# A decoder step on one Trainium2 core: the query tiles of the prompt attention in another order

## The chip, the core and the metric

The kernel runs on one core of one Trainium2 chip. The metric is the device time of one execution in microseconds (us); of several executions the median counts. The core has five engines with queues of their own: PE (TensorE, matrix products; PEld is its weight load), DVE (VectorE), ACT (ScalarE), POOL (GpSimd) and SP (SyncE, here only a queue of DMA transfers). They run side by side and wait for one another through semaphores.

## The reference

One step of a one-layer decoder on a prompt of 1024 tokens and on 8 sampled tokens with 4096 past positions each. The part that the change touches is the sparse attention of the prompt (8 query heads of 64 elements, 2 key-value heads), three branches over the same queries, mixed by gates. Since the prompt has 16 blocks of 64 and the 16 best are chosen, the selected branch is plain causal attention here.

```python
def masked_softmax(s, mask):
    s = jnp.where(mask, s.astype(jnp.float32), -1e30)
    m = jnp.max(s, axis=-1, keepdims=True)
    e = jnp.where(mask, jnp.exp(s - m), 0.0)
    return e / jnp.maximum(jnp.sum(e, axis=-1, keepdims=True), 1e-30)

def win_attend(qg, q_pos, k, v, k_pos, slopes):
    dist = (q_pos[:, None] - k_pos[None, :]).astype(jnp.float32)
    mask = (k_pos[None, :] >= 0) & (dist >= 0) & (dist <= WINDOW)
    s = jnp.einsum('bhgtd,bshd->bhgts', qg, k).astype(jnp.float32) * (NSA_HEAD_DIM ** -0.5) - slopes[None, :, :, None, None] * dist
    p = masked_softmax(s, mask)
    return jnp.einsum('bhgts,bshd->bhgtd', p.astype(v.dtype), v)

def nsa_merge(g, o_cmp, o_slc, o_win, dtype):
    o = g[0] * o_cmp + g[1] * o_slc + g[2] * o_win
```

`cmp_attend` (63 compressed rows) and `sel_attend` (all keys up to the query) have the same form. No query tile needs the result of another.

## The kernel before, in words

The program is a row of phases: load and norm, input projection, the gated linear attention, then `phase_attend` (the prompt's sparse attention, line 1594), `phase_sample` (the 8 sampled tokens, with the output projection in its last part) and the feed-forward phase. `phase_attend` and what follows it share one block, so each engine goes on to the sample phase as soon as its own queue of the attention is empty; between the phases before them all engines meet.

**Units.** The 1024 queries are 8 tiles of 128. A unit is one query tile `qt` with one pair of heads `gp`, twice, for both key-value heads; there are 16 units, two per query tile, in the order of the tuple `order_qt` (line 1610). `SU` lists them. Unit n has `ls = (qt + 1) * 128` selected keys, `lw` window keys (up to 640) and 63 compressed ones. That makes 319, 575, 831, 1087, 1343, 1471, 1599 and 1727 columns per head for `qt` 0 to 7, in (`tiles`, line 1638) 3, 5, 7, 9, 11, 12, 13 and 14 tiles of keys, and in (`chunks`, line 1619) 2, 2, 2, 3, 4, 4, 4 and 4 groups of score columns for each of the two g.

**What happens to a unit.** PE multiplies queries with keys (`score`, L1852). DVE adds the slope's distances, copies the scores from PSUM to SBUF and takes maxima (`reduce`, L1789 to L1800). ACT takes exponentials and sums (`exps`, L1726). DVE turns sums and gates into weights (`weigh`, L1809 to L1812). POOL multiplies the first key-value head's probabilities with them (L1707), ACT the second's (L1750). PE turns the probabilities tile by tile (`turn`, L1867), ACT and DVE move the turned tiles alternately out of PSUM (L1737, L1819), PE multiplies them with the values (`values`, L1880), ACT moves the result to `hT` (L1742), and SP stores it (L1697).

**Stages.** All engines walk the same loop `for n in range(-2, NSU)`. In stage n, PE turns and multiplies unit n while it scores unit n + 2; ACT meanwhile does the second half of the exponentials of unit n + 1 and the first half of unit n + 2. The work of the unit ahead is dealt out over the `J = stages(n)` steps of unit n by `share`. The turning of unit n + 1 waits for the last weighing of that unit on POOL (`normd`) and on ACT (`norma`), which is the last thing ACT does in stage n:

```python
            if j == 0:
                pe.wait_ge(normd, 2 * n + 2)
                pe.wait_ge(norma, 2 * n + 2)
```

Stages -2 and -1 have nothing to turn: they are the opening, with the scores of units 0 and 1 alone. Stages 14 and 15 have nothing to score: they are the close. In the close POOL also issues three gathers of cache rows for the sample phase (`gather_rows`, L1585), two of them behind a wait for the last turning of unit 13, and so ahead of the last two weighings. SP issues one twelfth of a copy of the cache (`pack_blocks`) ahead of each of its first 12 stores.

Of the kernel before, what the change touches and what calls it, by code (L numbers as in the profile page):

```python
# [1593 lines left out]
def phase_attend(nc, M, A, O, block):  # L1594
# [12 lines left out]
    sm = M.misc[:, 712:712 + 6 * NSLOT].rearrange("p (s b k) -> p s b k", s=NSLOT, b=3)  # L1607
    rc = M.misc[:, 736:736 + 6 * NSLOT].rearrange("p (s b k) -> p s b k", s=NSLOT, b=3)

    order_qt = (1, 3, 5, 7, 6, 4, 2, 0)  # L1610
    SU = [(qt, gp) for qt in order_qt for gp in range(2)]
    NSU = len(SU)

# [1879 lines left out]
def build(nc, A, O):  # L3493
    M = Mem()
    with ExitStack() as ctx:
        layout(nc, ctx, M)
        pool_rows = A["cache_nsa_kv"].shape[1] * PAGE
        M.packed = nc.dram_tensor("packed_rows", [pool_rows // 8, 8 * 2 * KVH * HD], FP32).ap()
        M.packed_blocks = nc.dram_tensor("packed_blocks", [pool_rows // 4, 4 * 2 * KVH * HD], FP32).ap()
        with nc.Block() as block_:  # L3500
            phase_load(nc, M, A, block_)
            phase_norms(nc, M, A, O, block_, Norm(nc, M, 0, None, M.nw[:, 0], 0))
        phase_project(nc, M, A, O)
        phase_mid(nc, M, A, O)
        end_of_stage(nc, M)
        M.nested = Nested(M)
        for name in ("mix_summed", "rows_back", "out_weights_loaded", "new_rows_product", "new_rows_moved", "rows_loaded",
                     "tail_on_scalar", "heads_joined"):
            M.sem(name)
        with nc.Block() as block_:  # L3510
            phase_attend(nc, M, A, O, block_)
            mix_views(M)
            mid_norm = Norm(nc, M, 1, M.rows[:, 0, :], M.nw[:, 1], 2)
            phase_sample(nc, M, A, O, block_, mid_norm)
            last_norm = Norm(nc, M, 2, M.rows[:, 0, :], None, 4)
            feed = Feed(nc, M, last_norm)
            phase_norms(nc, M, A, O, block_, mid_norm, feed)
            phase_ffn(nc, M, A, O, block_, feed)
            phase_norms(nc, M, A, O, block_, last_norm)
# [18 lines left out]
```

## Time and profile before

| | |
|---|---|
| median of 3 runs | 1753.68 us (1749.61 to 1754.86) |
| the profiled execution: time, span | 1750.74 us, 1749.0 us |
| mean granted TensorE clock | 0.982 of full speed |
| busy in the span: PE, PEld | 1677.5 us (96%), 1360.3 us (78%) |
| busy: DVE, ACT, POOL | 1100.1, 518.0, 831.3 us |
| the prompt attention | 382.8 to 643.1 us of the span |

A page gives the busy time of each engine, the groups of instructions with their mean duration, and for idle time the one that ended it. The timeline lists instructions in order of start; "[1.58 <-POOL ring L1707]" says that the engine had been idle for 1.58 us and that POOL's instruction of line 1707 ended that. "issue" is idle time with no releaser in the trace. PEclk is the granted clock: 1.00 is 2.4 GHz, 0.50 is 1.2 GHz.

### The profile page before, as it was taken

To read this page: it belongs to the slowest core of one execution; us is meant where nothing else is said; L and a number is where in the kernel's file an instruction comes from. 1 tells how busy PE (TensorE), PEld (TensorE's weight loads), DVE (VectorE), ACT (ScalarE), POOL (GpSimd) and SP (SyncE) were. 2 spreads that over 40 slices of the span, in tenths; PEclk is the share of its full clock that TensorE was granted. 3 is DMA by queue.
4 is the path that set the end of the run, shared out by engine and by line. 5 is a ranking of instruction groups with operands and counts; after the bars stand their busy time and mean duration, and the time that the engine had idled before them with its cause. 6 is when DMAs were issued, how large, how long until landed. Compare 5 with 4: busy or idle time off the path is not lost.

```text
span 1749.0 us, 24573 instructions
## 1 busy us (share of the span) xinstructions
PE 1677.5 (96%) x9278; PEld 1360.3 (78%) x9278; DVE 1100.1 (63%) x2113; ACT 518.0 (30%) x1100; POOL 831.3 (48%) x644
## 2 busy tenths in 40 slices
PE   8999999998999989999999989999999999999997
PEld 7888888774555557777788878888888888888886
DVE  5322110456776667766641169896789678968897
ACT  3311111348887752234222262200120012000202
POOL 3221221324444451423221189956684669476933
PEclk9999999989999989999999999999999999999998
DMA  5598893839444454845634451212021101211005
GB/s 155 145 261 255 238 276 90 245 126 273 148 148 139 139 171 171 294 159 217 230 125 119 160 190 39 73 49 73 1 73 52 70 23 51 73 49 49 1 1 194
DMA packets 172396, 233.53 MB, mean 134 GB/s; under 512 B 22488, under 2 KB 137096, under 8 KB 168120
## 3 DMA queue, kind: packets, MB, share of 16 engines
q1 hardware_dynamic: 162024, 181.64, 34.0%
q0 software_dynamic: 9216, 50.34, 8.0%
q8 instruction: 74, 1.21, 0.3%
q14 instruction: 42, 0.34, 0.1%
q10 hardware_dynamic: 1040, 0.00, 0.0%
HBM read 217.58 MB, written 102.45 MB: 183 GB/s over the span
## 4 chain that ended last, share of the span: by engine, by line
PE 63%; DVE 7%; issue 3%; POOL 2%; ACT 2%; another core or an unknown queue 0%; DVEq 0%
PE PS L3138 35%; PE PS L2218 6%; PE PS L2416 6%; PE PS L1852 4%; PE PS L1867 4%; PE PS L1880 4%; DVE Z L3198 1%; DVE Z L2598 1%; POOL X L3072 1%; DVE Z L437 1%; PE PS L412 1%; DVE Z L3158 1%; POOL Z L1707 1%; PE PS L506 1%; PE PS L2262 0%
## 5 line engine op out<-in xcount | busy, mean ns | idle before, releaser
L3198 DVE TENSOR_TENSOR Z<-PS,Z 128x516 f32<-128x516 f32 x432 | 288.4, 687 | 109.8 <-PE PS L3138 108.0
L2218 PE MATMUL PS<-Z 128*128 128x256 f32 x768 | 189.3, 396 | 3.4 <-issue 2.4
L2218 PEld LDWEIGHTS PS<-Z 128*128 128x128 f32 x768 | 144.1, 196 | 33.0 <-issue 13.1
L3138 PE MATMUL PS<-Z,X 128*128 128x258 f32 x584 | 137.2, 381 | 2.6 <-POOL X L3072 2.6
L3138 PE MATMUL PS<-srow,misc 128*128 128x258 f32 x560 | 133.4, 381 | 0.0
L3138 PEld LDWEIGHTS PS<-Z,X 128*128 128x128 f32 x584 | 110.7, 190 | 19.5 <-POOL X L3072 3.0
L1144 DVE TENSOR_TENSOR Z<-PS,Z 128x516 f32<-128x516 f32 x27 | 18.8, 696 | 159.4 <-PE PS L312 159.4
L3138 PEld LDWEIGHTS PS<-srow,misc 128*128 128x128 f32 x560 | 106.0, 190 | 15.8 <-DVE Z L3200 0.2
L3138 PE MATMUL PS<-srow,X 128*128 128x258 f32 x480 | 113.3, 380 | 0.0
L270 POOL TENSOR_TENSOR srow<-ring 128x512 f32<-128x512 f32 x15 | 21.2, 1411 | 190.6 <-PE PS L312 114.9
L3152 ACT ACTIVATE Z<-Z 128x2064 f32<-128x2064 f32 x16 | 30.8, 1925 | 247.1 <-DVE Z L3198 247.1
L3138 PEld LDWEIGHTS PS<-srow,X 128*128 128x128 f32 x480 | 90.8, 190 | 13.4
L3146 ACT ACTIVATE Z<-PS 128x516 f32<-128x516 f32 x16 | 9.6, 602 | 289.7 <-PE PS L3138 289.7
L1707 POOL TENSOR_SCALAR Z<-Z,misc 128x63 f32<-128x63 f32 (+8 forms) x48 | 58.3, 1230 | 65.7 <-DVE misc L1812 65.6
L1852 PE MATMUL PS<-Z 64*128 64x512 f32 (+3 forms) x384 | 84.0, 533 | 1.6 <-DVE misc L1789 0.9
L312 PE MATMUL PS<-hT,ring 128*128 128x258 f32 x352 | 79.5, 382 | 0.0
L312 PE MATMUL PS<-X,srow 128*128 128x258 f32 x352 | 79.0, 381 | 0.0
L312 PEld LDWEIGHTS PS<-hT,ring 128*128 128x128 f32 x352 | 66.3, 189 | 10.4 <-issue 0.4
L312 PEld LDWEIGHTS PS<-X,srow 128*128 128x128 f32 x352 | 66.5, 189 | 10.0
L975 ACT ACTIVATE Z<-PS 128x516 f32<-128x516 f32 x36 | 21.6, 601 | 167.7 <-PE PS L312 167.7
L3138 PE MATMUL PS<-Z,ring 128*128 128x258 f32 x288 | 68.8, 382 | 2.4 <-DVE Z L3198 2.4
L3138 PE MATMUL PS<-hT,ring 128*128 128x258 f32 x288 | 68.0, 381 | 2.3 <-DVE hT L584 2.3
(484 smaller groups left out, 3825.4 us busy)
## 6 DMA issues: line engine op xcount, KB each, us to landing
packed_rows<-in_cache_nsa_kv SPq DMA_DIRECT2D x32, 1280.0 KB, 14.9
packed_blocks<-in_cache_nsa_kv SPq DMA_DIRECT2D x16, 2560.0 KB, 11.5
X<-in_w_ff_down SPq DMA_DIRECT2D x12, 1024.0 KB, 5.2
ring<-in_w_in SPq DMA_DIRECT2D x9, 1024.0 KB, 5.2
X<-in_x_prompt SPq DMA_DIRECT2D x8, 1024.0 KB, 12.4
ring<-in_w_ff_up SPq DMA_DIRECT2D x8, 1024.0 KB, 5.3
Z<-in_w_ff_up SPq DMA_DIRECT2D x8, 1024.0 KB, 5.2
out_y_prompt<-X SPq DMA_DIRECT2D x16, 512.0 KB
```

The costliest lines, as they stand in the source:

```text
L270: pool.tensor_tensor(st.s1, block(w, 1, 0), block(w, 1, 1), ALU.add).then_inc(st.sums_r, 1)
L312: last = nc.tensor.matmul(M.PS[:, bank_of(M, n, e) + c, 0:CW], a[:, k, :], b[:, k, c * CW:(c + 1) * CW], start=e in (M1, M2, M5) and k == ...
L975: nc.scalar.activation(out, bank_view(M, n, e), ACT.Copy).then_inc(st_.act, 1)
L1707: last = pool.tensor_scalar(p_of(n, g, kvh)[:, c:c + w], p_of(n, g, kvh)[:, c:c + w], rc[:, m % NSLOT, br, kvh:kvh + 1], None, ALU.mult)
L1852: last = nc.tensor.matmul(M.PS[:, 2 * (cc % 2) + kvh, at:at + w], M.Z[r, Z_Q + 2 * gp + g, qt * P:(qt + 1) * P], k, start=True, stop=True)
L1867: last = nc.tensor.transpose(M.PS[0:w, 4 + gc % 2, (2 * kvh + g) * P:(2 * kvh + g + 1) * P], p_of(n, g, kvh)[:, c:c + w], M.ident[:, :])
L1880: last = nc.tensor.matmul(M.PS[d, 6 + n % 2, 0:2 * P], v, ptile[gc % 4][0:w, kvh * 256:kvh * 256 + 256], start=(j == 0), stop=(j == ngroup ...
L2218: last = nc.tensor.matmul(product(kind, v), w, x, start=(j == 0), stop=(j == 7))
L2416: last = nc.tensor.matmul(M.PS[:, mix_bank(n, e) + c, 0:256], a[:, k, :], x[:, k, 256 * c:256 * (c + 1)], start=e in (M1, M2, M5) and k == ...
L3138: last = nc.tensor.matmul(M.PS[:, N_.bank(n, e) + c, 0:HB], x[:, k, c * P:(c + 1) * P], y[:, k, :], start=e in (M1, M2, M5) and k == 0, st ...
L3152: nc.scalar.activation(x, x, ACT.Relu).then_inc(N_.relu, 1)
L3198: nc.vector.tensor_tensor(N_.part(out, e), N_.view(n, e), N_.part(old, e), ALU.add).then_inc(N_.dve, 1)
```

## The change

```diff
-    order_qt = (1, 3, 5, 7, 6, 4, 2, 0)
+    order_qt = (0, 2, 4, 6, 7, 5, 3, 1)
```

The units are the same 16, and each instruction of the attention is there before and after with the same operands, apart from the buffers that go by the unit's number. What moves is which unit stands in which stage. Pairs of stages (unit turned; unit scored) were (1;3) (3;5) (5;7) (7;6) (6;4) (4;2) (2;0) (0;none), and are (0;2) (2;4) (4;6) (6;7) (7;5) (5;3) (3;1) (1;none). The opening scores tile 0 in place of tile 1, and the close turns tile 1 in place of tile 0.

The opening on ACT, behind the table load. L1726 is the exponential, L1750 the weighing; `Z`, `srow` and `ring` are the buffers of the scores. Before:

```order
L1726 ACTIVATE Z,misc<-Z,misc 128x256 x2
L1726 ACTIVATE Z,misc<-Z,misc 128x63
L1726 ACTIVATE srow,misc<-srow,misc 128x256 x2
L1726 ACTIVATE srow,misc<-srow,misc 128x63
L1750 ACTIVATE srow<-srow,misc 128x256 x2
```

And now:

```order
L1726 ACTIVATE Z,misc<-Z,misc 128x128 x2
L1726 ACTIVATE Z,misc<-Z,misc 128x63
L1726 ACTIVATE srow,misc<-srow,misc 128x128 x2
L1726 ACTIVATE srow,misc<-srow,misc 128x63
L1750 ACTIVATE srow<-srow,misc 128x128 x2
```

The steps are the same, with half the columns in the selected and window branches.

The close on ACT, stage 14, from the result of unit 13 (L1742) to the last weighing (L1750 on `ring`). L1737 is the move of a turned tile. Before:

```order
L1742 ACTIVATE hT<-PS 128x2x128
L1726 ACTIVATE ring,misc<-ring,misc 128x128 x2
L1726 ACTIVATE ring,misc<-ring,misc 128x63
L1726 ACTIVATE ring,misc<-ring,misc 128x128 x2
L1726 ACTIVATE ring,misc<-ring,misc 128x63
L1737 ACTIVATE Z<-PS 63x512
L1750 ACTIVATE srow<-srow,misc 128x128 x2
L1750 ACTIVATE srow<-srow,misc 128x63
L1750 ACTIVATE ring<-ring,misc 128x128 x2
```

And now:

```order
L1742 ACTIVATE hT<-PS 128x2x128
L1726 ACTIVATE ring,misc<-ring,misc 128x256 x2
L1726 ACTIVATE ring,misc<-ring,misc 128x63
L1726 ACTIVATE ring,misc<-ring,misc 128x256
L1737 ACTIVATE Z<-PS 128x512
L1750 ACTIVATE srow<-srow,misc 128x256 x2
L1750 ACTIVATE srow<-srow,misc 128x63
L1726 ACTIVATE ring,misc<-ring,misc 128x256
L1726 ACTIVATE ring,misc<-ring,misc 128x63
L1737 ACTIVATE X<-PS 63x512
L1750 ACTIVATE ring<-ring,misc 128x256 x2
```

A move and the weighing on `srow` now stand between the last unit's exponentials, where they stood behind them.

The close on POOL, the difference of before and now, from the two gathers to the last weighing:

```order
 L1585 DMA Z<-packed_rows,idx 128x2048 x2
-L1707 TENSOR_SCALAR Z<-Z,misc 128x128 x2
-L1707 TENSOR_SCALAR Z<-Z,misc 128x63
-L1707 TENSOR_SCALAR ring<-ring,misc 128x128 x2
+L1707 TENSOR_SCALAR Z<-Z,misc 128x256 x2
+L1707 TENSOR_SCALAR Z<-Z,misc 128x63
+L1707 TENSOR_SCALAR ring<-ring,misc 128x256 x2
 L1707 TENSOR_SCALAR ring<-ring,misc 128x63
```

The gathers keep their place, and the two weighings behind them are those of 256 columns.

## Rows read from the trace of the kernel before

**Rows 1.** Windows over the attention: from, to, us; busy (instructions); PEclk, DMA, GB/s
```profile
382.80:396.71 13.91, 11.79 (x56) 7.19 (x57) 9.54 (x62) 11.45 (x43) 4.60 (x7) 0.63 0.54 208
396.71:456.05 59.34, 51.98 (x344) 29.39 (x345) 41.51 (x174) 49.11 (x137) 27.60 (x24) 0.94 0.80 242
456.05:537.77 81.72, 81.72 (x577) 46.46 (x578) 57.72 (x221) 66.40 (x150) 39.24 (x24) 1.00 0.43 136
537.77:610.22 72.45, 69.44 (x512) 41.66 (x512) 45.49 (x190) 57.08 (x148) 32.20 (x24) 1.00 0.49 153
610.22:631.01 20.79, 18.96 (x162) 12.53 (x160) 13.40 (x80) 18.14 (x69) 10.40 (x14) 1.00 0.20 65
631.01:643.13 12.12, 9.34 (x48) 5.29 (x48) 5.40 (x13) 6.05 (x23) 6.04 (x9) 0.73 0.81 282
```
**Rows 2.** Chain of waits, full clock: start, us, what
```profile
499.25 0.84 PE PS L1852 x4
500.09 1.03 PE PS L1867 x8
501.12 1.01 PE PS L1880 x8
```
**Rows 3.** Timeline of PE: first turning of units 0, 1, 2 and 4
```profile
396.71 0.33 PE L1867 MATMUL PS<-ident,Z 128*128 128x128 f32 x1 [1.58 <-POOL ring L1707]
396.88 0.27 PE L1867 MATMUL PS<-ident,ring 128*128 128x128 f32 x1
...
407.30 1.50 PE L1867 MATMUL PS<-ident,Z 128*128 128x128 f32 x8 [1.74 <-POOL Z L1707]
...
421.11 1.66 PE L1867 MATMUL PS<-ident,X 128*128 128x128 f32 x8 [2.48 <-POOL X L1707]
...
456.05 1.07 PE L1867 MATMUL PS<-ident,Z 128*128 128x128 f32 x8 [1.28 <-issue]
```
**Rows 4.** Timeline of DVE and ACT: a score copy, exponentials, weighings of tiles 1, 0
```profile
383.70 0.42 DVE L1789 CUSTOM_DVE_ANT_0 Z<-PS,srow 128x256 f32<-128x256 f32 x1 [0.72 <-PE PS L1852]
...
390.14 0.49 ACT L1726 ACTIVATE ring<-ring,misc 128x256 f32<-128x256 f32 x1
...
395.39 1.13 ACT L1750 ACTIVATE ring<-ring,misc 128x256 f32<-128x256 f32 x3
...
628.21 0.39 ACT L1726 ACTIVATE Z<-Z,misc 128x128 f32<-128x128 f32 x1
...
630.02 0.92 ACT L1750 ACTIVATE X<-X,misc 128x128 f32<-128x128 f32 x3
```
**Rows 5.** Timeline of PE: a bubble in stage 10, first turning of unit 13
```profile
580.08 0.66 PE L1867 MATMUL PS<-ident,Z 128*128 128x128 f32 x4 [0.73 <-DVE X L1819]
...
621.31 1.09 PE L1867 MATMUL PS<-ident,Z 128*128 128x128 f32 x8 [1.36 <-POOL Z L1707]
```
**Rows 6.** Timeline of POOL: a weighing of tile 1, and the close
```profile
394.39 2.26 POOL L1707 TENSOR_SCALAR ring<-ring,misc 128x256 f32<-128x256 f32 x3 [2.96 <-DVE misc L1812]
...
630.85 1.00 POOL L1585 DMA_INDIRECT Z<-packed_rows,idx  x1 [0.15 <-issue]
632.16 0.95 POOL L1585 DMA_INDIRECT Z<-packed_rows,idx  x1 [0.31 <-issue]
633.14 1.63 POOL L1707 TENSOR_SCALAR Z<-Z,misc 128x128 f32<-128x128 f32 x3
635.49 1.62 POOL L1707 TENSOR_SCALAR ring<-ring,misc 128x128 f32<-128x128 f32 x3 [0.72 <-DVE misc L1812]
```
**Rows 7.** Timeline, all engines: turnings of unit 15, and DVE and PE in the sample phase
```profile
637.43 0.42 PE L1867 MATMUL PS<-ident,ring 128*128 128x128 f32 x1
...
640.83 4.61 DVE L2598 STREAM_TRANSPOSE Z<-Z 128x1024 f32<-128x1024 f32 x4
...
645.53 4.87 PE L2218 MATMUL PS<-Z 128*128 128x256 f32 x11 [2.40 <-issue]
```
**Rows 8.** Windows behind the last scores, columns as in rows 1
```profile
637.00:640.20 3.20, 3.03 (x14) 2.37 (x16) 0.69 (x1) 0.87 (x2) 1.11 (x2) 0.50 0.95 343
```

## The prediction

> **What bounds the kernel now.** The order of the query tiles concerns only the prompt attention, so I began with the windows over it, cut at the stages' starts [rows 1]. The attention takes 260.3 us. In stages 4 to 7 PE is busy for all of 81.72 us and nothing else can matter. In the opening, in stages 0 to 3 and in the close PE is idle for part of the time, ACT is the busiest in the opening (11.45 of 13.91) and close to it in stages 0 to 3 (49.11 of 59.34), and the granted clock is not full (0.63, 0.94, 0.73). So a stage has one of two owners: PE where the tiles are large, the string ACT, DVE, POOL, PE where they are small.
>
> The total of PE's work is the same in any order. A new order can gain or lose only in what stands idle, in the half-speed stretches, and in the two ends. I therefore price each stage by its owner and compare with what it took.
>
> **PE's price of a stage.** Turning two tiles takes 1.03 us, their values 1.01, and four products of 512 columns 0.84 [rows 2]: 1.02 us per tile of keys, and a unit's scores (8 passes over its columns) c/300 us for c columns. With 0.2 us for each group of score columns, stages 4 to 7 come to 19.6 + 19.6 + 21.2 + 21.2 = 81.6, against 81.72 measured [rows 1]. The 0.2 is fitted to that sum.
>
> **ACT's price.** An exponential with its read takes 0.39 us for 128 columns and 0.49 for 256; three weighings 0.92 for tile 0 and 1.13 for tile 1 [rows 4]. This gives 1.6 + c/600 us for the six exponentials of half a unit and 0.6 + c/1200 for its weighing. With 0.5 per moved tile, 0.26 for the result, and 1.1 from the stage's first turning to the first move and from the last weighing to the next turning, stages 0 to 3 come to 10.7 + 12.2 + 14.3 + 15.1 = 52.3. They took 59.3 [rows 1, 3]. The other 7 us lie behind pauses of PE: it was idle for 1.74 and 2.48 us before units 1 and 2, and the first eight turnings behind them took 1.50 and 1.66 us, where behind 1.28 us of idle they took 1.07 [rows 3].
>
> **The change, part by part.**
>
> Opening: 13.9 us now [rows 1], with the clock at 1.2 GHz for most of it. With 319 in place of 575 columns, DVE's first maxima are ready 0.8 us sooner (the four copies take 0.42 each at 256 columns [rows 4], the first product comes sooner), the three sets of six exponentials ahead of the first turning are shorter by 0.43 each and the two weighings by 0.2 each [rows 4]: 2.5. The last weighing on POOL, 2.26 now, becomes 1.63 [rows 6], but ACT's string is the longer one, so that is covered. I take 2.8, between 2.5 and 3.2, the spare being PE's scores at half clock. Opening 11.1: **-2.8**.
>
> Stages 0 to 3, now (0;2) (0;2) (2;4) (2;4): ACT's price is 8.9 + 10.4 + 12.8 + 14.0, PE's 6.6 + 6.6 + 13.2 + 13.2. By owner 46.5. To this I add 6.1 of the 7 us of excess, since the pauses of PE grow (in stage 1 it has 6.6 us of work in 10.4), and a pause brings the slow clock back. The excess could be 3 or 10. Stages 0 to 3: 52.6, **-6.7**.
>
> Stages 4 to 7, now (4;6) (4;6) (6;7) (6;7): PE's price 18.15 and 20.6, twice each, with the 0.1 us by which the sum missed: 77.7, **-4.0**. ACT's price is 1 to 3 us lower in each.
>
> Stages 8 to 11, now (7;5) (7;5) (5;3) (5;3): PE's price is 20.8 and 17.1, twice each, 75.7. The present ones have a price of 68.3 and took 72.45 [rows 1]; of the 4.1 excess 3.2 lie in the two stages (4;2), where 4 groups of scores are dealt over 6 steps, so that the first step has none and PE turns into a PSUM bank that is not yet free (0.73 us in one place [rows 5]). A stage (5;3) has 6 groups for 6 steps. I take 1.6 of excess (bounds 0.5 and 4): 77.3, **+4.9**.
>
> Stages 12 and 13, now (3;1) (3;1): PE's price 11.9 each, ACT's about 12.7 and 10.5. In stage 12 POOL's weighing ends last already now (PE idle for 1.36 us behind POOL [rows 5]). The present stages have PE prices of 9.0 and took 20.8 together; I take 12.9 + 12.6 = 25.5, **+4.7**.
>
> Close: 12.1 us for two stages with tile 0 [rows 1]. In stage 14 the string is: first turning, move, result, four exponentials, move, weighing of the first half, two more exponentials (now behind that weighing, as the order shows), together 5.6 us; 0.75 for DVE's weights; then POOL's weighing of 2.26 in place of 1.62 [rows 6]: 8.8 in place of 6.15. POOL's two gathers (1.00 and 0.95) stand ahead of it, but with the first weighing of 2.26 behind them they end at about 5 us, so they stay covered. In stage 15 five tiles are turned and multiplied in place of three. Now this happens at 1.2 GHz (0.42 us for a turning [rows 7] that takes 0.27 at 2.4 GHz [rows 3], clock 0.50 [rows 8]), and the pause of PE ahead of it, with the last values of unit 14 waiting for ACT, only grows; so 9.5 us in place of 5.95. Close 18.3, **+6.2**.
>
> The POOL queue is passed by nothing: the third gather of the close has more time to land, not less. SP's stores and copies of the cache go with the units' ends; the twelfth copy starts some 12 us sooner, and nobody waits for it before the attention has ended. Behind the attention the order of events is unchanged: DVE starts its transposes right behind its last move (640.83), PE follows at 645.53 [rows 7], and both keep their distance from the last turning.
>
> **The sum**: -2.8 - 6.7 - 4.0 + 4.9 + 4.7 + 6.2 = +2.3 us. In short, the ascending half gets cheaper by what the descending half gets dearer, and the close loses a bit more than the opening wins. On the profiled execution's own time of 1750.74 that is 1753.0. The median of the three runs, 1753.68, is 2.9 us above that execution, and the runs spread over 5 us; on the median it is **1756.0**.
>
> **A rule on the clock.** The half clock in the close is what the rows show: 0.50 from 637.0 to 640.2 with PE busy for 3.03 of 3.20 us [rows 8]. The Trainium skill ("TensorE: Matmul & The Clock Gate", Part 1, section "What's actually happening") states that the throttled state is the default and that activity releases it. By that rule alone the five tiles of the new close, a longer stretch of work than three, could release the clock on the way. Stage 15 would then take about 7 us and the sum would be -0.2.
>
> **Rivals.**
>
> *The clock stays at 1.2 GHz longer, and the kernel is slower.* Place: stages 0 and 1. Before, dense products of 512 columns for unit 2 closed the opening, and the clock was full when unit 0 was turned (0.33 and 0.27 us a turning [rows 3]). Now these are 384 columns wide and the pause behind them is as long. If the clock is still half at that point, PE's 6.6 us each in stages 0 and 1 become 13, above ACT's 8.9 and 10.4, and cost up to 4 us in stage 0 and 2 in stage 1 until it is released; with a close of 10.5 in place of 9.5 the sum is +2.3 + 4.5 + 1 = +7.8: 1761. It decides once PE's work at half clock exceeds ACT's price. For it: the low clock of the opening [rows 1]. Against: once PE had such work, turnings at full speed came back within a stage.
>
> *The close and the first stages keep the full clock, and the kernel is faster.* Stage 15 at 6.5 (-3), excess of stages 0 to 3 at 3 (-3), the sample phase's first products at full clock (-2; they took 4.87 us for 11 at 645.53 [rows 7]), -5.7 in sum: 1748. For it: an early part with less to do. Against: each of these pauses is as long as those before which the clock fell.
>
> *Nothing but PE counts, and the order is neutral.* Stages of fixed work in another order: 0, 1753.7. Against: PE is idle for 21 us of the attention outside its prices. It is inside my own range.
>
> That the change does not do what it says is excluded: the order shows both ends exchanged.
>
> **Chances.** A measurement of this kernel can tell about 0.3% from no change, 5.3 us. My forecast (between -4 and +5) 0.66, the neutral order included; slower through the clock 0.22; faster through the clock 0.12. All of the forecast's case is within 0.3%. The range takes in the bounds of the excesses (-3, +4 in stages 0 to 3; -1, +2.4 in 8 to 11; -2.5, +1 in the close), which seldom fall together, and a bit of the spread of the runs: 1749 to 1762.
>
> **What would show it.** In the profile after: the first turning at 11.1 us from the attention's start (now 13.9), unit 4's at 63.7 (now 73.2), unit 8's at 141.4 (now 155.0), unit 12's at 218.7 (now 227.4), unit 14's at 244.2 (now 248.2), and the end at 262.5 (now 260.3). The gain stands at its largest, some 13 us, when unit 8 is turned, and is given back from there. Stage 14 is ended by POOL L1707. PEclk is below 1.00 in the opening, in the first stages and in the close. The forecast is wrong if the attention is shorter than 256 or longer than 267 us, or if the sample phase behind it takes another time than now.

## The result, and the profile after

The changed kernel takes **1759.95 us** (median of 7 runs, 1759.03 to 1762.17), the kernel before 1750.56 on the same chip (7 runs, 1748.53 to 1754.86). The ratio is 1.0056, 95% interval 1.0045 to 1.0066: **slower by 0.56%**, 9.4 us. That is more than the 0.3% that a measurement can tell from no change. The profiled execution took 1759.95 us with a span of 1758.2, against 1750.74 and 1749.0. The mean clock is 0.981 against 0.982. Of the 9.2 us between the two spans, +9.8 lie in the attention up to the sample phase (below), +2.5 ahead of it (its first product starts at 385.34 in place of 382.84) and -3.1 in the phases behind it. No run tests the last two, so that the 9.4 of the timed runs and the 9.8 of the trace are so close is in part chance.

The same windows over the attention as in [rows 1], for the changed kernel, cut where units 0, 4, 8, 12 and 14 are first turned (from, to, us; busy (instructions) of PE, PEld, DVE, ACT, POOL; PEclk, DMA share, GB/s):

```profile
385.34:397.23 11.89, 9.56 (x61) 7.19 (x61) 7.24 (x62) 9.71 (x43) 3.46 (x7) 0.58 0.56 210
397.23:452.92 55.69, 42.99 (x276) 26.34 (x277) 36.40 (x174) 42.61 (x133) 22.95 (x25) 0.88 0.87 265
452.92:534.24 81.32, 79.33 (x545) 44.51 (x545) 55.16 (x210) 64.61 (x148) 37.81 (x24) 0.98 0.44 137
534.24:611.85 77.61, 76.80 (x547) 43.99 (x545) 52.20 (x205) 61.50 (x150) 35.53 (x25) 1.00 0.45 143
611.85:638.28 26.43, 24.66 (x193) 15.87 (x193) 14.57 (x66) 21.98 (x71) 13.66 (x15) 1.00 0.16 51
638.28:654.07 15.79, 12.43 (x80) 7.48 (x80) 5.95 (x17) 8.10 (x25) 6.38 (x8) 0.89 0.64 217
```

Read the first number behind each pair and subtract the one of [rows 1]. From the first score to the sample phase's first product (line 2218) the changed kernel needs 272.5 us (385.34 to 657.83), the one before 262.7 (382.8 to 645.53 [rows 7]). I call this distance **the attention up to the sample phase**, and use it for every kernel below.

| part | before | after | measured | predicted |
|---|---|---|---|---|
| opening | 13.91 | 11.89 | -2.0 | -2.8 |
| stages 0 to 3 | 59.34 | 55.69 | -3.65 | -6.7 |
| stages 4 to 7 | 81.72 | 81.32 | -0.4 | -4.0 |
| stages 8 to 11 | 72.45 | 77.61 | +5.2 | +4.9 |
| stages 12, 13 | 20.79 | 26.43 | +5.6 | +4.7 |
| close, up to the sample phase | 14.52 | 19.55 | +5.0 | +6.2 |
| sum | | | **+9.8** | **+2.3** |

The first three rows, where the gain was to be, gained 6.1 us in place of 13.5. The losses came nearly as forecast, 15.8 in place of 15.8. That the losses agree so well is in part chance: single parts are off by +0.3, +0.9 and -1.2. So the place to look is stages 0 to 4. PE there, first turnings of units 1, 2, 3, 4 and 5 in the changed kernel:

```profile
406.20 1.97 PE L1867 MATMUL PS<-ident,Z 128*128 128x128 f32 x8 [3.27 <-POOL Z L1707]
420.37 1.97 PE L1867 MATMUL PS<-ident,X 128*128 128x128 f32 x8 [4.69 <-POOL X L1707]
437.35 0.33 PE L1867 MATMUL PS<-ident,Z 128*128 128x128 f32 x1 [1.50 <-POOL ring L1707]
452.92 1.57 PE L1867 MATMUL PS<-ident,Z 128*128 128x128 f32 x8 [2.77 <-POOL Z L1707]
473.13 1.06 PE L1867 MATMUL PS<-ident,X 128*128 128x128 f32 x8 [0.50 <-issue]
```

The bracket tells how long PE had been idle and who ended it. Before units 1 and 2 that was 1.74 and 2.48 us [rows 3] and is now 3.27 and 4.69; before unit 4 it was 1.28 and is 2.77. The duration in the second column is, in the rows with x8, that of eight turnings: 1.06 at 2.4 GHz, 1.97 at 1.2 GHz. So each of the three long pauses is followed by work at half clock, the last for only part of the eight. The windows of stages 0 to 3 show how much of each stage that was (before, then after):

```profile
396.71:407.30 10.59, 8.19 (x57) 4.59 (x57) 8.14 (x34) 9.79 (x33) 4.49 (x7) 1.00 0.63 214
407.30:421.11 13.81, 11.34 (x64) 5.95 (x65) 8.92 (x35) 11.34 (x33) 7.41 (x7) 0.88 1.06 300
421.11:439.35 18.24, 17.03 (x113) 9.78 (x113) 11.57 (x50) 13.75 (x36) 6.70 (x6) 0.91 0.96 284
439.35:456.05 16.70, 15.42 (x112) 9.07 (x113) 12.88 (x56) 14.22 (x35) 9.01 (x6) 1.00 0.54 165
```

```profile
397.23:406.20 8.97, 5.23 (x37) 2.90 (x37) 6.47 (x33) 7.97 (x32) 3.07 (x7) 0.97 0.51 220
406.20:420.37 14.17, 9.48 (x49) 5.93 (x49) 7.34 (x34) 9.57 (x32) 5.76 (x7) 0.74 1.00 267
420.37:437.35 16.98, 15.48 (x97) 9.69 (x97) 10.59 (x51) 11.98 (x35) 5.71 (x6) 0.83 1.08 323
437.35:452.92 15.57, 12.80 (x96) 7.82 (x97) 11.99 (x58) 13.09 (x34) 8.41 (x7) 1.00 0.73 225
```

Stage 1 (0;2) has less to turn than the old (1;3) and takes longer, 14.17 against 13.81, with the clock at 0.74.

**Why PE waits there.** Each pause is ended by POOL, and POOL started late. DVE around the end of stage 1 (a score copy that waited for PE, the last of the copies, then the weights of unit 2), and POOL behind it:

```profile
414.33 0.56 DVE L1789 CUSTOM_DVE_ANT_0 ring<-PS,srow 128x384 f32<-128x384 f32 x1 [0.81 <-PE PS L1852]
...
416.54 0.08 DVE L1789 DVE_READ_ACCUMULATOR2_ANT misc<- 128x1 f32 x1
416.65 0.17 DVE L1800 TENSOR_TENSOR misc<-misc 128x6 f32<-128x6 f32 x1
...
417.16 0.17 DVE L1812 TENSOR_TENSOR misc<-misc,gt 128x6 f32<-128x6 f32 x1
```

```profile
417.42 2.90 POOL L1707 TENSOR_SCALAR X<-X,misc 128x384 f32<-128x384 f32 x3 [8.41 <-DVE misc L1812]
```

Unit 2's last exponential ended at 412.0. Its weights could follow at once, but in DVE's queue they stand behind the copies of unit 3's scores, which wait for PE. They come at 417.3, and POOL's three instructions, of up to 384 columns, end at 420.32, 0.05 before PE's first turning. In so short a stage there is too little of unit 1 (tile 0) to turn to cover that. The half clock has a part in it too: PEclk was 0.50 from 406.2 to 412.0 us, so PE came later to the scores of unit 3 for which these copies wait.

### The profile page after: what moved, and what is told of

Read it like the earlier page. It is cut to its first block, busy times and chain, and to the rows that moved or that the text cites. A ratio compares the mean times of both kernels' runs of the same rounds, so it can differ in the third digit from the quotient of the medians.

```text
span 1758.2 us, 24573 instructions
## 1 busy us (share of the span) xinstructions
PE 1680.1 (96%) x9278; PEld 1363.4 (78%) x9278; DVE 1100.7 (63%) x2113; ACT 518.5 (29%) x1100; POOL 828.7 (47%) x644
## 4 chain that ended last, share of the span: by engine, by line
PE 65%; DVE 6%; issue 2%; POOL 2%; ACT 2%; another core or an unknown queue 0%; DVEq 0%
PE PS L3138 35%; PE PS L2218 8%; PE PS L2416 6%; PE PS L1867 4%; PE PS L1852 4%; PE PS L1880 4%; DVE Z L3198 1%; POOL ring L1707 1%; POOL X L3072 1%; DVE Z L437 1%; DVE Z L3158 1%; PE PS L412 1%; PE PS L506 1%; DVE Z L2598 0%; PE PS L2262 0%
## 5 line engine op out<-in xcount | busy, mean ns | idle before, releaser
L312 PEld LDWEIGHTS PS<-X,srow 128*128 128x128 f32 x352 | 67.6, 193 | 10.5
L312 PEld LDWEIGHTS PS<-hT,ring 128*128 128x128 f32 x352 | 66.3, 189 | 10.3 <-issue 0.4
L3138 PE MATMUL PS<-Z,ring 128*128 128x258 f32 x288 | 68.7, 382 | 2.4 <-DVE Z L3198 2.4
## 6 DMA issues: line engine op xcount, KB each, us to landing
packed_blocks<-in_cache_nsa_kv SPq DMA_DIRECT2D x16, 2560.0 KB, 11.9
```

Of the source, the lines that this page charges most:

```text
L312: last = nc.tensor.matmul(M.PS[:, bank_of(M, n, e) + c, 0:CW], a[:, k, :], b[:, k, c * CW:(c + 1) * CW], start=e in (M1, M2, M5) and k == ...
L3138: last = nc.tensor.matmul(M.PS[:, N_.bank(n, e) + c, 0:HB], x[:, k, c * P:(c + 1) * P], y[:, k, :], start=e in (M1, M2, M5) and k == 0, st ...
```

## The experiments

All are built on the two kernels. "Ratio" is to the kernel before on the same chip, with its 95% interval. The sample phase and the feed-forward phase behind the attention, the same instructions in every kernel, took 1094.4 to 1107.0 us over the profiled executions. So the attention up to the sample phase is the finer measure: 262.7 us before, 272.5 after. It is read from one execution of each kernel. Two of the edits below (DVE's weights in the old order, the last weights of the close in the new one) leave stages 0 to 3 as they are; the same instructions took 60.0 us there against 59.3, and 55.6 against 55.7.

**The interior of the order alone.** Both ends stay as they were:

```diff
-    order_qt = (1, 3, 5, 7, 6, 4, 2, 0)
+    order_qt = (1, 2, 4, 6, 7, 5, 3, 0)
```

> The order 1, 2, 4, 6, 7, 5, 3, 0: the change with tiles 0 and 1 exchanged, so the middle is that of the change and the two ends are those of the kernel before. Theory 1 (the 9.4 us are lost in the ascending half, where stages with a small tile are too short for the weighing of the next, larger unit, PE pauses, and the clock falls): the jump from 1 to 2 is smaller than from 0 to 2, but the stages are still short, so 2 to 5 us above the kernel before, about 1754. Theory 2 (the close with tile 1 in place of tile 0 costs it: stages 14 and 15 take 15.8 in place of 12.1 us and the sample phase starts 1.4 us later behind it): the ends are the old ones, so within 1 us of the kernel before, 1750.5.

Measured: 1756.51 us, ratio 1.0020 (1.0005 to 1.0034). The attention up to the sample phase took 266.6, +3.9 of the +9.8. So the interior costs 3.9 and the exchange of the ends another 5.9, of which the close is 5.1, stages 12 and 13 are 1.8, stages 0 to 3 are 0.9 and the opening is -2.0. The stages 4 to 11 took the same to 0.01 us as in the changed kernel, so stages depend on their own pair of units and not on how the attention began. The pause before unit 2 was 2.12 us here. The 2 to 5 us of theory 1 came out for the interior. That the ends cost more still, most of it in the close, neither theory had said.

**DVE's weights ahead of the copies.** In a step with the second half of the weights, DVE takes them before that step's copies, where `J` is even:

```diff
+                early = J % 2 == 0 and i == J // 2 and 0 <= n + 1 < NSU
+                if early:
+                    weigh(n + 1, 1)
...
-                if i == J // 2 and 0 <= n + 1 < NSU:
+                if not early and i == J // 2 and 0 <= n + 1 < NSU:
```

On the changed kernel:

> The changed kernel, and on DVE the weights of unit n + 1 (second half) stand ahead of the score copies of their step, where the number of steps is even (tiles 0, 2, 4, 5). In the changed kernel unit 2's last exponentials are done at 412.0 us and its weights are ready at 417.3, behind score copies, and POOL starts only then. Theory 1: POOL starts 3 to 5 us sooner in stage 1 and some 1 us sooner in stages 0 and 3, the pauses of PE ahead of units 1, 2 and 4 shrink from 3.3, 4.7 and 2.8 us to about 1 to 2, and the clock falls less often: 4 to 7 us faster than the changed kernel, about 1754. Theory 2 (the close): no change beyond 1 us, 1760.

Measured: 1756.96 us, ratio 1.0012 (0.9997 to 1.0028) in place of 1.0056. Stages 0 to 3 took 50.1 us in place of 55.7, with the clock at 0.93 in place of 0.88. POOL's weighing of unit 2 started 7.1 us after the first turning of unit 1 (406.44), in place of 11.2; POOL, then PE:

```profile
413.57 2.90 POOL L1707 TENSOR_SCALAR X<-X,misc 128x384 f32<-128x384 f32 x3 [4.42 <-DVE misc L1812]
```

```profile
417.42 1.94 PE L1870 MATMUL PS<-ident,X 128*128 128x128 f32 x8 [2.80 <-POOL X L1707]
```

The pause before unit 2 shrank from 4.69 to 2.80, and the clock still fell (1.94 for eight); before units 1 and 4 the pauses were 3.03 and 2.07, more than the 1 to 2 expected. Part of the gain was given back later: stage 13 took 14.31 in place of 12.69 and stage 15 7.98 in place of 7.09, together 2.5, with the clock at 0.88 in stage 13 where it had been 1.00, behind the same pause of 1.11 us. That leaves 269.2 up to the sample phase, 3.3 less than the changed kernel.

The same edit on the kernel before, as a control:

> The same edit on DVE in the kernel before, as a control. There tiles 1 and 3, whose stages have the pauses, have 3 and 5 steps, so the edit does nothing in them, and works only in the stages of tiles 5, 4, 2 and 0. Theory 1: 0 to 2 us faster, 1749 to 1750.5, from stages 10 and 12. Theory 2: no change. If it is slower, earlier weights on DVE hold up the score copies, which would also spoil the reading of the edit in the changed kernel.

Measured: 1752.67 us, ratio 1.0001 (0.9986 to 1.0017); 263.2 up to the sample phase. It gains nothing in the old order, from the stages in which it acts (those of tiles 5, 4, 2 and 0). The old order's stages 0 to 3 have an odd number of steps and the edit leaves them alone, so whether late weights cost time there too is not shown.

**Descending order.** No short stage at the beginning at all:

```diff
-    order_qt = (1, 3, 5, 7, 6, 4, 2, 0)
+    order_qt = (7, 6, 5, 4, 3, 2, 1, 0)
```

> The order 7, 6, 5, 4, 3, 2, 1, 0: no ascending half at all. Theory 1: the opening grows from 13.9 to some 22 us (three sets of exponentials of 4.5 us, two weighings of 2 us), but 14.7 us of PE's scores are done in it, and stages 0 to 3 lose their 8 us of pauses and slow clock; the attention takes about 252 us in place of 260: 4 to 9 us faster than the kernel before, about 1743. Theory 2: the opening with the largest tile costs 8 us, the close is the old one: 5 us slower than before or more, 1756.

Measured: 1760.25 us, ratio 1.0036 (1.0022 to 1.0050); 272.5 up to the sample phase, where some 252 for the attention had been expected. The opening took 29.8 us. I had expected 22, and that was the miss: the first turning waited for a whole string of large work.

```profile
385.26 4.73 PE L1852 MATMUL PS<-Z 64*128 64x512 f32 x12 [0.71 <-PEq L1195]
...
408.18 1.13 PE L1852 MATMUL PS<-Z 64*128 64x512 f32 x4 [0.56 <-DVE misc L1789]
415.03 0.47 PE L1867 MATMUL PS<-ident,Z 128*128 128x128 f32 x1 [5.72 <-POOL ring L1707]
```

The first twelve products took 0.39 us each, the full clock having them at 0.21 (0.84 for four [rows 2]). Between the last scores and the first turning PE is idle for 5.72 us, until POOL has weighed a unit of 1727 columns. The stages behind gained nothing against the price of PE: stages 0 to 3 and 4 to 7 took 83.9 and 70.9 us, by the prediction's price 81.9 and 68.7.

**Starting at tile 2.** The smallest two tiles both at the end:

```diff
-    order_qt = (1, 3, 5, 7, 6, 4, 2, 0)
+    order_qt = (2, 4, 6, 7, 5, 3, 1, 0)
```

> The order 2, 4, 6, 7, 5, 3, 1, 0: the smallest tiles both last. The descending order showed an opening of 29.8 us for tile 7, since PE scores two units there at half clock. For tile 2 I expect 15.8 us (1.9 above tile 1). Theory 1 (short stages with small tiles ahead of large ones cost pauses): stages 0 to 3 are now those of tiles 2 and 4, so two short stages fewer in the ascending half; stages 12 to 15 are (1;0)(1;0)(0)(0), with some 3 us of pauses more in the close. In sum within 2 us of the kernel before, to the faster side: 260 to 263 from the attention's start to the first product of the sample phase. Theory 2 (the ends decide): 262.7 plus the opening's 1.9.

Measured: 1752.04 us, ratio 1.0027 (1.0012 to 1.0043); 266.1 up to the sample phase, +3.4. The opening took 16.6, 2.7 more than with tile 1. Without the short stages (0;2) it is 6.4 us shorter than the changed kernel, and yet it stays behind the old order. The opening is 2.7 of the 3.4 us; the close is not longer (13.8 us up to the sample phase, 14.5 before).

**Keeping PE busy through the pauses.** Products whose result nobody reads stand ahead of the wait for POOL in stages that begin with a pause, and so fill a part of that pause. They go to an unused part of a PSUM bank, so the results are the reference's:

```diff
             if j == 0:
+                for _ in range({1: 12, 2: 18, 3: 5, 4: 10, 15: 6}.get(n, 0)):
+                    nc.tensor.matmul(M.PS[:, 6 + (n + 1) % 2, 256:512], M.ident[:, :], M.Z[:, Z_Q, 0:256], start=True, stop=True)
                 pe.wait_ge(normd, 2 * n + 2)
```

On the changed kernel:

> The changed kernel with PE kept at work in its pauses: ahead of the wait of units 1, 2, 3, 4 and 15 it multiplies 12, 18, 5, 10 and 6 times the identity with 256 columns into an unused part of PSUM, which nobody reads. Theory 1a (half of what the ascending half loses is the slow clock behind each pause, not the pause itself): the clock stays at 2.4 GHz from unit 1 on, stages 1, 2 and 4 shrink by 2 us each, the attention up to the first product of the sample phase takes about 266 in place of 272.5 us. Theory 1b (the pauses count, the clock is covered by ACT, which is behind anyway): under 2 us of gain, 271 or more. If these products delay the turning, stages get longer in place of shorter.

Measured: 1759.36 us, ratio 1.0054 (1.0031 to 1.0078); 272.9 up to the sample phase. A miss in the dose: one such product takes two instructions and about 0.45 us (36 instructions in 8.04 us for the 18), so 12 and 18 of them were longer than the pauses, and PE came late to the turning. Stage 0 took 12.0 us in place of 9.0. The clock stayed at 1.00 from 408 us, and yet this run alone decides nothing.

On the kernel before, with 6, 9, 4, 4 and 4 products ahead of units 1, 2, 3, 4 and 15:

> The kernel before with the same products in the pauses ahead of units 1, 2, 3, 4 and 15 (6, 9, 4, 4 and 4 of them). Theory 1a: the half clock behind the pauses ahead of units 1 and 2 and in the last stage goes, which is 1.7 us each: the attention to the first product of the sample phase takes 258 in place of 262.7 us, the time 1746 in place of 1750.5. Theory 1b: no gain, 262 or more.

Measured: 1745.1 us, ratio 0.9992 (0.9975 to 1.0009); 264.9 up to the sample phase. The old order has shorter pauses, so this was too much again: stage 0 took 12.34 in place of 10.59. Stage 15, with the clock kept, took 3.63 in place of 5.96.

The changed kernel with about half of them, 6, 9, 2, 5 and 3:

> The same products in the pauses of the changed kernel, but as many as fit (each took 0.44 us at 2.4 GHz in the longer version, twice what I had reckoned, and delayed units 1 to 3): 6, 9, 2, 5 and 3 ahead of units 1, 2, 3, 4 and 15. Theory 1a (half clock behind the pauses costs as such): stage 1 13.0 or less (14.2 in the changed kernel), stage 2 14.9 (17.0), stage 4 18.6 (20.2), 5 us less from the attention's start to the first product of the sample phase, 267.5. Theory 1b (covered): 271 or more.

Measured: 1748.47 us, ratio **1.0003** (0.9988 to 1.0018), and 263.95 up to the sample phase in place of 272.5, 3.5 better than expected. Stages 1, 2 and 4 took 11.3, 14.3 and 18.6 us. PE around the first turning of unit 1 (the row of line 1862 is the added products), and the windows of the attention:

```profile
404.01 2.86 PE L1862 MATMUL PS<-Z,ident 128*128 128x256 f32 x12
407.35 1.09 PE L1869 MATMUL PS<-ident,Z 128*128 128x128 f32 x8 [0.49 <-POOL Z L1707]
```

```profile
386.49:398.38 11.89, 9.65 (x60) 7.20 (x61) 7.24 (x62) 9.71 (x43) 3.46 (x7) 0.57 0.56 216
398.38:448.50 50.12, 47.70 (x320) 30.67 (x320) 36.32 (x174) 42.42 (x133) 22.95 (x25) 1.00 0.96 288
448.50:528.20 79.70, 77.70 (x544) 43.85 (x544) 55.13 (x210) 64.49 (x148) 37.83 (x24) 1.00 0.45 143
528.20:605.90 77.70, 76.89 (x547) 44.03 (x546) 52.24 (x205) 61.50 (x150) 35.58 (x25) 1.00 0.45 143
605.90:632.30 26.40, 24.64 (x193) 15.85 (x194) 14.60 (x66) 21.98 (x71) 13.63 (x15) 1.00 0.16 51
632.30:646.70 14.40, 12.53 (x86) 7.55 (x86) 5.94 (x17) 8.09 (x25) 6.35 (x8) 1.00 0.69 234
```

PE does more work in stages 0 to 3 (47.70 us busy in place of 42.99), waits for the same engines, and the stages take 50.12 in place of 55.69. The busy times of DVE, ACT and POOL are the same to 0.3 us. The only other thing that changed is the clock: 1.00 in place of 0.88. A part of what it gives comes by way of DVE: POOL's weighing of unit 2 started 8.3 us after the first turning of unit 1 in place of 11.2, since unit 3's scores came sooner. Stages 4 to 7 gain 1.6 and the close 1.4; stages 8 to 13, where nothing was added, stay within 0.1. This is the run that shows the cause.

The kernel before with 3 products ahead of unit 1, 4 ahead of unit 2, 2 ahead of unit 15:

> The kernel before with 3, 4 and 2 products in the pauses ahead of units 1, 2 and 15, as many as fit. Theory 1a: stage 1 12.5 (13.8 now), stage 2 16.5 (18.2 now), 259 to 260 us to the first product of the sample phase, 3 us faster than the kernel before and the fastest so far. Theory 1b: 262 or more.

Measured: 1743.03 us, ratio **0.9962** (0.9941 to 0.9983), the fastest of all; 261.4 up to the sample phase. Its windows:

```profile
384.39:398.21 13.82, 9.48 (x56) 5.58 (x57) 9.34 (x62) 11.41 (x43) 4.96 (x7) 0.88 0.54 209
398.21:455.23 57.02, 53.42 (x359) 31.16 (x359) 42.03 (x174) 48.93 (x137) 27.30 (x24) 0.97 0.83 252
455.23:537.00 81.77, 81.77 (x577) 46.51 (x578) 57.77 (x221) 66.39 (x150) 39.23 (x24) 1.00 0.43 136
537.00:609.40 72.40, 69.40 (x513) 41.60 (x513) 45.44 (x188) 57.05 (x148) 32.21 (x24) 1.00 0.49 153
609.40:631.80 22.40, 20.54 (x163) 13.66 (x161) 13.44 (x81) 18.26 (x69) 10.46 (x14) 0.92 0.20 60
631.80:641.60 9.80, 7.75 (x52) 4.51 (x52) 4.00 (x11) 6.05 (x23) 5.97 (x9) 1.00 0.83 269
```

The gain lies between the two theories (259 to 260, or 262 and more). Stages 1 and 2 came as expected, 12.4 and 16.6. Stages 0 to 3 gained 2.3 us and stages 14 and 15 another 2.3, but PE then waited for 4.17 us in place of 2.40 for the sample phase, which takes 1.8 back. Stages 12 and 13, where nothing was added, took 22.4 in place of 20.8 with the clock at 0.92. The trace shows 1.3 us of gain up to the sample phase, the ratio 6.6 (3.0 to 10.3). Where the rest comes from stays open: it lies in the phases behind (1095.8 us in place of 1103.5), whose time varies by as much from kernel to kernel.

**The last weights of the close.** In the changed kernel a weighing stood between unit 15's exponentials; here it stands behind them, for that unit alone:

```diff
-                if i == J // 2 and 0 <= n + 1 < NSU:
+                if i == J // 2 and 0 <= n + 1 < NSU - 1:
...
+                if i == J // 2 and n + 1 == NSU - 1:
+                    weigh(n + 1, 0)
```

> The changed kernel, and on ACT the weighing of the last unit's first half stands behind the last two exponentials and not ahead of them (one instruction group in stage 14). My step for the close said that stage 14 is the string exponentials, weights, POOL's last weighing, and that the weighing on ACT now stands in it. If so, stage 14 shrinks from 8.7 to 7.7 us, and everything before it is unchanged; in the time 1 us, 1759 (hard to tell from 1760). If POOL's gathers or its first weighing of 2.26 us hold the last one, stage 14 stays at 8.7.

Measured: 1753.4 us, ratio 1.0042 (1.0029 to 1.0055); 270.0 up to the sample phase, 2.5 less. Stage 14 took 7.66 in place of 8.70, and stage 15 5.72 in place of 7.09. The first turning of unit 15, here and in the changed kernel:

```profile
645.83 0.33 PE L1869 MATMUL PS<-ident,Z 128*128 128x128 f32 x1 [0.82 <-POOL ring L1707]
```

```profile
646.98 0.33 PE L1867 MATMUL PS<-ident,Z 128*128 128x128 f32 x1 [1.85 <-POOL ring L1707]
648.42 0.48 PE L1867 MATMUL PS<-ident,Z 128*128 128x128 f32 x1 [0.35 <-DVE X L1819]
```

Behind 0.82 us of idle the clock stayed full to the end. Behind 1.85 us it fell 1.4 us later (0.33 us, then 0.48). So an exponential order that saved 1.0 us of waiting brought 1.4 more from the clock.

**All three together** on the changed kernel: early weights, the close in the other order, and 5, 5, 2, 4 and 2 products:

> The new order with the three edits together: early weights on DVE, the close reordered on ACT, and 5, 5, 2, 4 and 2 products in the pauses ahead of units 1, 2, 3, 4 and 15. If the causes add: 9.8 us above the kernel before less 3.2 + 1 in the ascending half by the weights, some 4 by the clock, 1 in the close: 263 to 264 us to the first product of the sample phase, level with the kernel before (262.7), the time within 0.1% of it. If the order had a loss of its own beyond these, it stays 4 us or more above it.

Measured: 1744.75 us, ratio 0.9980 (0.9965 to 0.9995); 262.6 up to the sample phase, against 262.7 before. All that the change had lost in the attention against the unedited old order is back. Beside the products alone (263.95) the other two edits bring only 1.3 us: most of what they won alone (3.3 and 2.5 us) overlaps with what the clock gives. Stages 0 to 3 took 50.35 us, no less than with the products alone (50.12).

## Why the prediction was wrong, point by point

The forecast, no change within 0.3%, was wrong. The case that happened had a chance of 0.22. The time, 1760, is inside the range and 4 us above the number, which is partly luck: the number stood on a median of 1753.68 for the kernel before, and next to the changed kernel that took 1750.56. The change itself was forecast at +2.3 and measured at +9.4; the attention, 268.7 us, is beyond the 267 that the text itself named as the limit.

**The step that failed** is "To this I add 6.1 of the 7 us of excess". The excess of the old stages was carried over as a sum, while its cause, a pause of PE and the half clock behind it, grows when PE has less to do. The prediction said itself that the pauses grow, and still took less than the 7. By owner the four stages were priced at 46.5. They took 55.7, an excess of 9.2, near the upper bound that I gave (10). With the clock kept they took 50.1, so 5.6 of the 9.2 went with the half clock and 3.6 stayed as waits. The two can't be parted cleanly: DVE's earlier weights gave the same 50.1 with the clock at 0.93, and both edits together 50.35. At half clock unit 3's scores come late, with them DVE's copies and the weights behind them, and so the pause grows.

**The second step that failed** is "PE's price" for stages 4 to 7 with nothing added but 0.1. The first of them follows a short stage: unit 4 was turned behind a pause of 2.77 us with the clock down, and stages 4 to 7 took 81.3 in place of 77.7. With the clock kept it was 79.7: of the 3.6, 1.6 is the clock. The other 2.0 are not explained by a run of their own; the window shows PE busy for 77.70 of 79.70, so they are idle time of PE, which the price by owner did not hold. These two terms, 3.1 and 3.6 us, are most of the 7.5 by which the sum missed. (The sum's own 77.7 should be 77.6, which changes nothing.)

**The order by itself costs near what the sum said.** Compare the two kernels with the smaller doses of added products, 263.95 against 261.36: the new order costs 2.6 us where the sum said 2.3. Part by part it is -1.9, -6.9, -2.1, +5.3, +4.0 and, for the close with its onset, +4.2, against -2.8, -6.7, -4.0, +4.9, +4.7 and +6.2. The parts are off by up to 2 us each, so that the sums agree is luck. The old order's clock was not quite full there (0.97 and 0.92 in stages 0 to 3 and 12, 13, the latter 1.6 us longer than before), so at full clock throughout the order would cost up to some 2 us more. Of the 9.8 us, then, 5 to 7 are the half clock and 3 to 5 the order, an estimate from these traces. The timed runs of these two kernels on one chip, medians 1748.47 and 1743.03, stand 5.4 us apart.

**The opening** was forecast at 11.1 and took 11.9; the direction and most of the size held.

**Stages 8 to 11** (77.3 forecast, 77.6 measured) and **12, 13** (25.5 and 26.4) held. These are the places where the owner's price was checked against stages of the same kind, and where the clock is full.

**The close** was forecast at 18.3 and took 15.8, plus 1.4 more than before until the sample phase's first product. Stage 14 was right: 8.8 forecast, 8.70 measured, ended by POOL's weighing of 256 columns as described. Stage 15 was forecast at 9.5 all at half clock and took 7.09:

```profile
648.40:651.40 3.00, 2.98 (x14) 2.28 (x16) 0.69 (x1) 1.18 (x3) 0.00 (x0) 0.51 0.81 240
651.40:654.10 2.70, 2.67 (x22) 1.12 (x18) 1.59 (x2) 0.00 (x0) 0.00 (x0) 1.00 0.49 175
657.80:661.00 3.20, 3.17 (x8) 2.55 (x9) 3.17 (x5) 0.00 (x0) 0.98 (x1) 0.56 0.00 0
```

The clock was down for 3 us, came back while the five tiles of unit 15 were at work, and was down again for the sample phase's first products. The Trainium skill ("TensorE: Matmul & The Clock Gate", Part 1, section "What's actually happening") says that activity releases the throttle; by that rule I had put stage 15 at about 7 us. The trace agrees, and I had been wrong to set it aside here. A longer stretch of work than three tiles isn't needed for it: with tile 0 in stage 15, all at half clock before (5.96 us), the same work behind the same pause of 1.22 us took 5.27 with the interior alone and 4.61 in the control of the weights, PEclk 0.68 in both. The statement that the sample phase keeps its distance was off by 1.4 us. DVE's transposes do follow its last move as before (653.12, with 4.7 us from there to PE's first product in both kernels), but with PE at full speed its last values end sooner, and it waits longer.

**The rivals.** The first, the clock, is the one that happened, and its price (+7.8, 1761) is close to the +9.4 and the 1760 measured. In size that is partly luck: it had nothing for stages 4 to 7, which missed by 3.6, and 10.5 us for stage 15, which took 7.09. Its place was only partly right. It named stages 0 and 1 with the clock still down from the opening. In fact unit 0 was turned at full speed (0.97 in stage 0), and the clock fell anew in stages 1, 2 and 4 behind POOL. Where it falls differs between executions: in the kernel with the last weights of the close moved, the same until stage 14, stages 0 and 1 had 0.83 and 0.82 and took 10.22 and 12.86 us in place of 8.97 and 14.17, the same sum. The second, a full clock in the close and the first stages, did not happen by itself: PEclk is 0.88 and 0.89 there. The added products made it happen, and then the changed kernel took as long as the one before (1.0003), not less. The neutral order is refuted by the time itself (1.0045 to 1.0066). With the clock kept, 2.6 us remain up to the sample phase, and the intervals of the two kernels with products (0.9988 to 1.0018, 0.9941 to 0.9983) don't meet. Its "idle for 21 us" is time above PE's price and holds half clock too; PE's idle time by [rows 1] is 17.1 us.

## What to carry to other kernels

In a pipeline over units of unequal size, ask of each stage whether the smaller unit being finished covers the serial string (exponentials, weights, weighing) of the larger one behind it; where it does not, TensorE's pause costs itself and then the half clock behind it, here together 9.2 us over four stages, 5.6 of which went once the clock was kept. Where such a pause can't be avoided, a few products that nobody reads, fewer than the pause holds, give most of the second back; too many cost as much as they save. Work that the engine's own half clock makes late (here DVE's weights behind the score copies) belongs to the same loop, so two cures for it don't add up.

## What the runs showed of the hardware

**No length of pause separates full from half clock in these rows.** Eight turnings took 1.50 us behind a pause of 1.74 and 1.66 behind 2.48 [rows 3], 1.57 behind 2.77 and 1.97 behind 3.27. But in the kernel with the interior alone a pause of 2.29 us ahead of unit 1 left the whole of stage 1 at PEclk 1.00. Behind the next, 2.12 us, eight turnings went at full speed and the next eight, 3.1 us later, took 1.87:

```profile
412.35 1.06 PE L1867 MATMUL PS<-ident,Z 128*128 128x128 f32 x8 [2.29 <-issue]
423.50 1.06 PE L1867 MATMUL PS<-ident,X 128*128 128x128 f32 x8 [2.12 <-POOL X L1707]
...
426.63 1.87 PE L1867 MATMUL PS<-ident,X 128*128 128x128 f32 x8
```

And a shorter pause is enough. Unit 13 of the old order is turned behind 1.36 us of idle. Before, stage 13 kept 1.00 [rows 5] and took 9.7 us; with 3, 4 and 2 added products, none of them near, it took 11.3 at 0.85:

```profile
620.47 1.09 PE L1869 MATMUL PS<-ident,Z 128*128 128x128 f32 x8 [1.36 <-POOL Z L1707]
...
622.12 1.97 PE L1869 MATMUL PS<-ident,Z 128*128 128x128 f32 x8
```

The length of the pause alone doesn't decide, and the fall can come over a microsecond behind it, so its cost is better given as a range. What else decides is not shown here.

**Turnings do run faster at the full clock.** The Trainium skill ("TensorE: Matmul & The Clock Gate", Part 4, "PE-mode transpose") says that the full clock doesn't engage for TensorE's transpose mode. Here eight of the kernel's `nc.tensor.transpose` in a row, which the trace lists as MATMUL, took 1.06 us at PEclk 1.00 and 1.97 us at half clock. The measurement decides for these fp32 transposes: the throttle slows them as it slows other products.

**An fp32 product of 256 columns, 128 by 128, is two instructions of 0.22 to 0.24 us each**: 12 instructions in 2.86 us for 6 products, 36 in 8.04 us for 18. Counting it as one is why the first two doses were too large.
